# Scale-vector products of the opening moved from VectorE to TensorE, and the first four tiles worked in two pairs

## The reference

```python
cs = jax.nn.silu(c)
mod = jnp.matmul(cs, ada_w[layer]) + ada_b[layer]
sh_m, sc_m, g_m, sh_f, sc_f, g_f = jnp.split(mod, 6, axis=-1)
h = rmsnorm(x, norm_mix_g) * (1.0 + sc_m) + sh_m
p = jnp.matmul(h, w_in)
```

## Time and profile before

| | us |
|---|---|
| median of three runs | 2001.44 |
| the profiled execution | 2000.84 |
| its span in the trace | 1999.1 |
| PE busy | 1924.0 (96%) |
| first real matmul of the first layer starts | 35.75 |
| last matmul of tiles 0 to 3 starts | 62.64 |

### The profile page before, as it was taken

One profiled execution on the slowest core, in us unless ns is written; L12 is line 12 of the kernel. 1 busy time (PEld: TensorE's weight loads), 2 busy tenths in 40 slices (PEclk: granted clock), 3 DMA queues, 4 the chain that ended last, 5 costly groups with the idle time before them and its releaser, 6 DMA issues.

```text
span 1999.1 us, 25116 instructions
## 1 busy us (share of the span) xinstructions
PE 1924.0 (96%) x8696; PEld 1549.9 (78%) x8696; DVE 1049.7 (53%) x1593; ACT 449.1 (22%) x766; POOL 1184.4 (59%) x907
## 2 busy tenths in 40 slices
PE   5999999999999999999999999999997899999998
PEld 4787868888888887667788888886774688888886
DVE  7566266666655453566766653244858553233222
ACT  3302342121110022442212111013127421111100
POOL 3743326788887956325687887743550256666673
PEclk7999999999999999999999999998999999999999
DMA  7432223555555422111455553321220023222332
GB/s 304 176 116 75 95 95 106 179 195 192 189 193 187 162 97 84 54 43 64 158 192 205 186 195 106 105 89 59 84 74 11 22 85 103 96 94 94 103 108 74
DMA packets 67374, 242.21 MB, mean 121 GB/s; under 512 B 7498, under 2 KB 7882, under 8 KB 67314
## 3 DMA queue, kind: packets, MB, share of 16 engines
q1 hardware_dynamic: 65536, 237.01, 34.1%
q10 hardware_dynamic: 1778, 4.37, 0.6%
HBM read 239.25 MB, written 2.10 MB: 121 GB/s over the span
## 4 chain that ended last, share of the span: by engine, by line
PE 88%; DVE 5%; ACT 3%; issue 2%; DMA 2%; POOL 1%; SPq 0%; ACTq 0%; DVEq 0%; POOLq 0%
PE gemm L445 23%; PE gemm L446 23%; PE gemm L447 23%; PE gemm L472 2%; PE gemm L474 2%; PE gemm L473 2%; DMA w_raw<-wstream 2%; PE mix L648 1%; PE gemm L801 1%; PE mix L445 1%; DVE sq_acc L1336 1%; PE mix L446 1%; PE mix L447 1%; PE mix L986 1%; PE gemm L815 1%
## 5 line engine op out<-in xcount | busy, mean ns | idle before, releaser
L429 POOL TENSOR_TENSOR w_lo<-w_raw,w_hi 128x1024 fp32r<-128x1024 f32 x302 | 735.2, 2435 | 25.2
L445 PE MATMUL gemm<-h_hi,w_hi 128*128 128x512 f32 x1616 | 634.2, 392 | 21.4 <-DVE h_lo L1157 14.8
L447 PE MATMUL gemm<-h_hi,w_lo 128*128 128x512 f32 x1616 | 630.7, 390 | 0.0
L446 PE MATMUL gemm<-h_lo,w_hi 128*128 128x512 f32 x1616 | 630.6, 390 | 0.0
L426 POOL TENSOR_TENSOR pool_gate<-pool_gate 128x1 f32<-128x1 f32 x298 | 118.1, 396 | 743.7 <-PE gemm L447 603.4
L445 PEld LDWEIGHTS gemm<-h_hi,w_hi 128*128 128x128 f32 x1616 | 304.6, 189 | 90.5 <-issue 22.1
L427 POOL TENSOR_SCALAR w_hi<-w_raw 128x1024 fp32r<-128x1024 f32 x302 | 343.9, 1139 | 17.5 <-DMA w_raw<-wstream 17.5
L447 PEld LDWEIGHTS gemm<-h_hi,w_lo 128*128 128x128 f32 x1616 | 304.4, 188 | 63.6
L446 PEld LDWEIGHTS gemm<-h_lo,w_hi 128*128 128x128 f32 x1616 | 304.6, 189 | 62.6
L1051 DVE CUSTOM_DVE_ANT_0 ada_raw<-ada_raw,c_act 128x1024 f32<-128x1024 f32 x128 | 215.5, 1699 | 110.1 <-DMA ada_raw<-adastream 110.1
L447 PE MATMUL gemm<-p_hi,w_lo 128*128 128x512 f32 x528 | 205.4, 389 | 0.0
(11 more groups left out here) (339 smaller groups left out, 1976.7 us busy)
## 6 DMA issues: line engine op xcount, KB each, us to landing
w_raw<-wstream SPq DMA_DIRECT2D x302, 512.0 KB, 3.5
ada_raw<-adastream SPq DMA_DIRECT2D x128, 512.0 KB, 4.4
a_early<-adastream SPq DMA_DIRECT2D x8, 1024.0 KB, 12.0
out<-x_res SPq DMA_DIRECT2D x8, 256.0 KB, 2.2
c_act<-c_in ACTq DMA_DIRECT2D x2, 512.0 KB, 7.3
x_res<-x_in SPq DMA_DIRECT2D x2, 512.0 KB, 6.4
x_res<-x_in ACTq DMA_DIRECT2D x2, 512.0 KB, 9.1
b_dist<-const_in ACTq DMA_DIRECT2D x1, 512.0 KB
```

Source lines behind the costliest of these rows:

```text
L429: pool.tensor_tensor(wlo[s][:], raw[:, u % RAW, :], whi[s][:].bitcast(F32), ALU.subtract).then_inc(w_split, 1)
L445: pe.matmul(out_ap, w_h, r_h, start=first, stop=False)
L446: pe.matmul(out_ap, w_h, r_l, start=False, stop=False)
L447: return pe.matmul(out_ap, w_l, r_h, start=False, stop=last)
```

## The change

Block k of the scale rows is stored in the input array as 128 x 128 blocks laid out as matmul weights, so that PE can form the 128 scale values of block k with eight accumulating matmuls of one column (`scale_sums(k)`), weights `a_early[:, 2k+1, ...]`, moving operand one column of silu(c) laid out along partitions (new columns `c_col`, put through Silu by ACT). DVE keeps only the shift product. The gain is then formed from the PSUM result. In DVE's loop `first_low(k)` now comes first in its turn instead of last. ACT waits for `first_scaled` alone. On PE the chunks k = 0..3 are first applied to tiles 0 and 1 only, then to tiles 2 and 3, then k = 4..7 to all four; `scale_sums` stand between.

```diff
+            def scale_sums(k):
+
+                pe.wait_ge(ada_first[k], 16)
+                if k == 0:
+                    pe.wait_ge(sig("c_cols"), 1)
+                if k >= 2:
+                    pe.wait_ge(ada_used, 2 * k - 2)
+                for b in range(KT):
+                    mm = pe.matmul(M[1 - k % 2][:, k:k + 1], ada_early[:, 2 * k + 1, b * P:(b + 1) * P], rms[:, 16 + b:17 + b],
+                                   start=b == 0, stop=b == KT - 1, skip_group_check=True)
+                mm.then_inc(sig("first_scale"), 1)
+
+            def opening_tiles():
...
+                for ks, us in ((range(4), (0, 1)), (range(4), (2, 3)), (range(4, KT), (0, 1, 2, 3))):
+                    for k in ks:
+                        if us[0] == 0 and k + 2 < KT and k != 4:
+                            scale_sums(k + 2)
+                        if us[0] == 2 and k == 2:
+                            scale_sums(6)
+                        pe.wait_ge(h_ready, k + 1)
+                        for u in us:
...
+            scale_sums(0)
             pe.wait_ge(const_in_sem, 16)
             bc[0] += 1
             bcast(rstdps, bc[0])
             keep_warm(WARM[2])
+            scale_sums(1)
...
-            tiles("even_in", 2, wide=4)
+            opening_tiles()
+            for u in range(4):
+                tile_chunk(N0["even_in"] + 4 + u, u % SPL, u, 1 + G0["even_in"][u])
...
-            def first_modulation(k):
+            def first_shift(k):
 
                 dve.wait_ge(ada_first[k], 16)
-                for u, m in ((0, k), (1, KT + k)):
-                    product_sum(ada_early[:, 2 * k + u, :], C1, col("ada_b", m), modv[:, m:m + 1])
-                dve.wait_ge(ada_used, 2 * k + 2)
-                dve.scalar_tensor_tensor(out=acol[:, k:k + 1], in0=modv[:, KT + k:KT + k + 1], scalar=1.0,
-                                         in1=col("norm_mix_g", k), op0=ALU.add, op1=ALU.mult).then_inc(sig("first_gain"), 1)
+                product_sum(ada_early[:, 2 * k, :], C1, col("ada_b", k), modv[:, k:k + 1])
+
+            def first_gain(k):
+
+                dve.wait_ge(sig("first_scale"), k + 1)
+                dve.scalar_tensor_tensor(out=acol[:, k:k + 1], in0=M[1 - k % 2][:, k:k + 1], scalar=rms[:, 24 + k:25 + k],
+                                         in1=col("norm_mix_g", k), op0=ALU.add, op1=ALU.mult).then_inc(ada_used, 1)
...
-            first_modulation(0)
+            link(dve.tensor_scalar(rms[:, 24:32], col("ada_b", KT, KT), 1.0, None, ALU.add))
+            first_shift(0)
             rms_n[0] += 1
             ready(inverse_rms(4, rms_n[0]))
-            first_modulation(1)
+            first_gain(0)
             spread()
             first_scaled(0)
+            first_shift(1)
+            first_gain(1)
             first_scaled(1)
             for k in range(KT):
+                first_low(k)
                 if k + 2 < KT:
-                    first_modulation(k + 2)
+                    first_shift(k + 2)
+                    first_gain(k + 2)
                     first_scaled(k + 2)
-                first_low(k)
...
+            act.wait_ge(cols_loaded, 16)
+            act.activation(rms[:, 16:24], col("c_col", 0, 8), ACT.Silu).then_inc(sig("c_cols"), 1)
             act.preload_act_table(ACT.Sqrt)
...
-            act.wait_ge(cols_loaded, 16)
...
-                act.wait_ge(sig("first_gain"), k + 1)
                 act.wait_ge(sig("first_scaled"), k + 1)
```

More of the change, by code:

```diff
@@ L53 @@
         ("oconv_w", 32), ("oconv_b", 8), ("onorm_g", 8), ("fconv_w", 132), ("fconv_b", 44),
-        ("final_g", 8), ("g_attn", 8), ("kv_g", 1), ("g_ffn", 8), ("g_final", 8), ("eps", 1), ("gate_b", 2)]
+        ("final_g", 8), ("g_attn", 8), ("kv_g", 1), ("g_ffn", 8), ("g_final", 8), ("eps", 1), ("gate_b", 2), ("c_col", 8)]
 COL = {}
@@ L580, in _ @@
             mm.then_inc(norm_sum, 1)
+            def scale_sums(k):
[9 more added lines that the diff above has]
+            def opening_tiles():
+                n = N0["even_in"]
+                for u in range(4):
+                    pe.wait_ge(gfree[u], G0["even_in"][u])
+                for ks, us in ((range(4), (0, 1)), (range(4), (2, 3)), (range(4, KT), (0, 1, 2, 3))):
[6 more added lines that the diff above has]
+                        for u in us:
+                            if k == 0 and u % 2 == 0:
+                                pe.wait_ge(w_split, n + u + 2)
+                            s = (n + u) % SPL
+                            mm = three(G[u][:], whi[s][:, k * P:(k + 1) * P], wlo[s][:, k * P:(k + 1) * P],
+                                       Hhi[:, k, :], Hlo[:, k, :], k == 0, k == KT - 1)
+                            if k == KT - 1:
+                                mm.then_inc(pe_done, 1)
+            scale_sums(0)
             pe.wait_ge(const_in_sem, 16)
@@ L2157, in prepare @@
     adastream[0:16] = adastream[0:16].reshape(2, 8, 128, 1024).transpose(1, 0, 2, 3).reshape(16, 128, 1024)
+    for k in range(8):
+        w = i["ada_w"][0][:, 1024 + 128 * k:1152 + 128 * k]
+        adastream[2 * k + 1] = w.reshape(8, 128, 128).transpose(1, 0, 2).reshape(128, 1024)
     crow = np.stack([i["c"].reshape(1024), i["c_2"].reshape(1024)])
@@ L2169, in prepare @@
     put("g_attn", i["g_attn_2"]); put("kv_g", i["kv_norm_g_2"]); put("g_ffn", i["g_ffn_2"]); put("g_final", i["g_final_2"])
+    put("c_col", i["c"])
     cols[:, COL["eps"]] = EPS
```

## The result

| | before | this |
|---|---|---|
| median (runs) | 2001.81 us (4) | 2055.81 us (4) |
| lowest to highest | 2000.59 to 2006.43 | 2051.33 to 2057.58 |
| profiled execution, its span | 2000.84, 1999.1 | 2057.17, 2055.4 |
| first tile matmul starts | 35.75 | 29.04 |
| last matmul of tiles 0 to 3 starts | 62.64 | 70.26 |

The ratio is 1.0268 [1.0252, 1.0284]: 54 us slower. The forecast was 2010.0 with a range up to 2014. The sign was right, the size and the range were wrong.

A forecast was written before the change was run, and what follows sets the result against it. PE, busy 96% of the span, was taken as the bound, idle in the opening awaiting DVE's `h_lo`. The opening's end moving from 62.9 to 72.7 (+9.8), less 1.2, gave +8.6 on median 2001.44: 2010.0 us, range 1998 to 2014.

The forecast's parts named there:

- Whatever the end of tiles 0 to 3 moves by, I carry to the end: After the opening: PE busy 34.00 of 34.00 us from 66 to 100, so the opening's shift passes on one to one.
- the line on ACT: Opening: ACT gains a Silu of 128x8, due by 16.13; given no cost, each us late costs one.
- the start of the first tile: Opening: first tile matmul starts at 29.7 instead of 35.75, 6.0 us earlier.
- T: PE's six matmuls of a pair of tiles for one k: 2.6 us at half clock or 1.4 at full.
- S: One `scale_sums` on PE, eight one-column matmuls in 16 records: 3.6 us at half clock, 1.8 taken at full.
- the opening's end: Last matmul of tiles 0 to 3: 72.7 against 62.9 before, +9.8 us, or +8.6 after the allowance.
- The allowance of 1.2 us: First pass over k: taken off for one T or S there that meets the full clock.
- S0: First `scale_sums` in PE's opening order, ahead of the spread, which it delays by 2.0 us.
- Rival B: Opening: clock falls in the one-column sums but comes back inside the first pass; +1.9 to +7, middle +4.5, 2006; chance 0.28.
- A: The forecast itself: half clock through most of the first pass; +7 to +13 us, 2008 to 2014; chance 0.52.
- C: Opening: clock up from the dummies on and never falls, not slower; -3.7 us, 1997.7, up to 2000.4; chance 0.17.
- D: Opening: only DVE's saving counts, one-column work slips under the tile matmuls' time; -12 us, 1989; chance 0.03.

The follow-up runs named there:

- The spare columns alone: Kernel before with eight columns that nothing reads added to `cols` (440 to 448), nothing else: 2046.31 us, ratio 1.0237.
- 456 columns: Changed kernel with eight more columns that nothing reads in `cols`, a shift of 64 bytes instead of 32: 2026.7 us, ratio 1.0139 against before.

## Why the prediction was wrong

- **The step that failed** is "Whatever the end of tiles 0 to 3 moves by, I carry to the end", and ahead of it the line on ACT, in which the new `c_col` columns cost only their Silu ("so I give it nothing"). The diff's first hunk makes a buffer 32 bytes longer, and the sum took 0.227 us per tile matmul as a property of the instruction. It is a property of where its two operands lie (0.2267 us before, 0.2333 with the shift). The missing term is 47 us worked out, 46.0 by the spans of the two profiles with and without the shift (2055.4 - 2009.4). The spare columns alone give 41.5 by their span (2040.6 - 1999.1), 5.4 less than the 46.9 of 7104 x 0.0066. Comparing the n-th tile matmul of the one with the n-th of the other, 3.1 of the 5.4 are given back between 63 and 296 us (from 185 to 200 the mean clock is 1.00 for 0.89 in before) and 2.3 between 1260 and 1672 us.
- **Right: the start of the first tile**, 29.04 for 29.7. But the prediction gave the gain to the change as a whole; the run with DVE's order alone shows that 6.1 of the 6.7 us come from it.
- **Right: the clock.** It fell inside the 32 one-column records and stayed at 0.50 through pass 1; the matmuls of T 0.43 apart, S 3.41 for 3.6, DVE waiting at the gain. No idle time went ahead of the fall: PE has none between 13.97 and 28.06, it is busy 2.00 of 2.00 us while the clock falls (26 to 28) and 3.00 of 3.00 at 0.50 (44 to 47).
- **Right within its allowance: the opening's end**, 70.26 for 72.7 less 1.2; +7.6 against +8.6. That it lies so near is in part luck. The allowance of 1.2 us stood for a T or S at full clock in the first pass, and there was none. Instead the first tile came 0.7 earlier, the first pass took 49.69 - 29.04 = 20.65 us for 21.2, and the clock came back after three matmuls of the second pass for nine, so that its first twelve took 3.2 us for 4.6. One sum is off: 21.6 + 3.6 - 1.0 is 24.2 and not 24.5 for the end of the dummies (23.86 measured). The first steps were near: S0 counted from 16.13 for 3.6 us to 19.7, and it started at 15.70, took 3.55, and the spread followed at 19.11. Of the two rates, 0.43 is what the trace has at half clock; 0.227 is the 0.23 of the earlier trace rows with one more digit and holds without the shift (0.2267), while this kernel had 0.2333. Rival B happened too: with 456 columns the clock came back after two T, and the last of 96 started at 64.32; B's sum has its end at 64.8, its start at 64.6. Without the shift the whole change costs 4.0 us by the ratio and 6.0 by the medians, near B's +4.5, and its profiled execution is an A. So the mechanism in the opening is right, and which of A and B a given execution takes is open.
- **Rivals C and D did not happen** (their 21.8 and 2.72 us are 96 and 12 tile matmuls at 0.227), and none of the rivals had its place outside the opening: that is what the range lacked. The list of signs spoke of a stretch behind 66 us that takes back the shift, not of one that adds to it.

## What to carry to other kernels

A diff that lengthens or adds a buffer can change every matmul that reads something allocated behind it (32 bytes took the pitch here from 0.2267 to 0.2333 us, 256 bytes left it at 0.2267): work out the distances between stationary and moving operands before and after, put small new data into free columns (those of `rms` left the pitch at 0.2267) or at the end, and look first at the pitch of an instruction that the change does not touch. Work that PE does with one column belongs where PE would be idle; between dense matmuls it is paid in full (3.41 us for eight at half clock, 1.84 at full), and in the changed kernel a low clock stayed low through it (0.50 in 35 to 38 and in 44 to 47). Before a product is moved to another engine, try the order of what is there: here it gave 6.1 of the 6.7 us of earlier start.

## What the runs showed of the hardware

- A 128x512 matmul of this kernel with its 128x128 load starts 0.2267 us after the one before when moving and stationary operand lie a multiple of 256 bytes apart (311 x 256, and 256 off that), and 0.2333 when the distance is 32 or 96 off one. At 64 off it is 0.2289 with `h` or `p` moving (64 past) and 0.2333 with the weights moving (64 short). With everything moved by 32 it stays at 0.2267. At 128 it was not measured. Why is not shown.
- PE's clock fell from 1.00 to 0.50 while PE was busy without a gap in one-column matmuls (2.00 of 2.00 us in 26 to 28 of the changed kernel, at a mean of 0.68). The mixture of tile matmuls and one-column sums behind it ran on at 0.50 (44 to 47 us in the changed kernel), rose to 1.00 by itself (0.96 in 38 to 41 with 456 columns), and stayed at 1.00 where dummies stood ahead (1.00 in 35 to 38 and in 44 to 47).
- The twelve executions of the change without its shift lay in groups, 4.2 to 4.5 us apart, with nothing in the program different. Stretches at half clock far behind the change differ between profiled executions: from 1330 to 1420 us the mean clock is 0.94 in before, 0.91 with all buffers moved and 0.89 in the change without its shift.
